# Gated delta stage of a two-block network: another spread of projections, norms and squares over a head, and two masked products for six copies

## The chip, the cores and the metric

The kernel runs on one core of a Trainium2 chip. The time is the device time of one execution in microseconds (us), the median of several runs. The core's engines have queues of their own and meet at semaphores: TensorE (PE, matrix products into eight PSUM banks), VectorE (DVE), ScalarE (ACT), GpSimd (POOL) and SyncE (SP, which issues the DMAs).

## The reference

The reference is a whole network of two blocks on 512 tokens of width 1024. The change is in one part of its first layer, the mixer with the gated delta rule. Four heads of width 128 each take four projections of the same input (query 0, key 1, value 2, gate 3). Query, key and value pass a causal convolution of four taps and a silu; query and key are brought to unit length; then the delta rule runs over four chunks of 128 tokens:

```python
g_qkv = jax.nn.silu(causal_dwconv(jnp.concatenate([g_q, g_k, g_v], -1), conv_g))
h_g = gated_delta_chunkwise(l2_norm(g_q), l2_norm(g_k), g_v, log_decay, beta)
y_g = head_rms_norm(h_g, g_norm) * jax.nn.silu(g_gate)

# in gated_delta_chunkwise, for each chunk
a_mat = where(strict, beta * kk * decay, 0) + eye        # unit lower triangular
sol = triangular_solve(a_mat, [v * beta, k * beta * exp(G)])
# and over the chunks
v_new = u - w @ state
o = q_dec @ state + attn @ v_new
state = g_last * state + k_dec.T @ v_new
```

## The kernel before

All work of the first layer's mixer is laid out by hand. `delta` (L2057) writes one list of instructions for each engine, and what order they have in the code is their order on the engine. Head h has a `body(h)` on each of PE, ACT, POOL and DVE (h = 0, 1, 2), and head 3 a `last_body`. While head h is solved and recurs, the next head (n = h + 1) is prepared and the one after (f = h + 2) is begun.

A projection is cut into eight units; one unit is the three 128x512 products of L190 to L192 (the float32 operands are split in a high and a low part). A head's body has two parts on PE:

- The levels. The triangular matrix is inverted blockwise, in six levels. A level has two short products, one into bank b4 (Y) and one into bank b6 (Z); ACT copies Y out of PSUM between them (`copy_y`), DVE takes Z up after them. Levels 1 to 4 work on 32x32 blocks (L2218), level 5 (`level_32`, L2239, L2248, L2249) on pairs of these, level 6 (`level_64`, L2256, L2262) on 64x64. These products are short and each waits for the other engines, so `fill(l, i)` puts units of other projections behind the Y product (i = 0) and behind the Z product (i = 1) of level l. For level 5 and 6 DVE first spreads the compact 32x32 blocks of T and U into the wide tiles `T_wide` and `U_wide` (L2701 four copies, L2703 two).
- The recurrence (`recur`), over four chunks, with `fill_chunk(c)` in the middle of chunk c.

Besides there are for the next head: `norms` (two 128x512 float32 products that sum squares, L2188, L2189), `roots` on ACT (four activations, L2424 to L2427), `unit` on DVE (L2666, L2667), `keys` on PE (key times key, key times query, key transposed, L2182, L2177), `scores` and `first_level` on DVE, and `turn_v` on PE (the value transposed).

Before the change, the gate projection of head n fills eight places in the levels (four for head 0), and the recurrence takes up query and key of head f and the value of head n, six units to a chunk. In head 2 there is no head f, so that only the value's eight units are left, two to a chunk. `norms` stand between levels 3 and 4, `keys` between level 6 and the recurrence. The squares for the norms are two activations of ACT. `split_high` (ACT, L154) and `split_low` (POOL, L163) split the weights of each projection in the two parts before it.

Of the kernel before, what the change touches and what calls it, by code (L numbers as in the profile page):

```python
# [20 lines left out]
P = 128  # L21
# [12 lines left out]
        ("reset", T), ("rcount", 2 * T), ("sel", 6 * P), ("small_levels", 32 * 5), ("small_ident", 32)]  # L34
# [2022 lines left out]
def delta(k, weights, out_tiles):  # L2057
# [23 lines left out]
     k_turned, v_turned, kdb_ready, vb_ready, kk_done, arg_ready, dec_ready, eg_ready, masked, at_ready, db_ready, qd_ready, t_ready, bt_ready, u_first, u_ready, a_ready, b0_ready, nat_ready, u_done, zeroed,  # L2081
# [3 lines left out]
         "k_turned v_turned kdb_ready vb_ready kk_done arg_ready dec_ready eg_ready masked at_ready db_ready qd_ready t_ready bt_ready u_first u_ready a_ready b0_ready nat_ready u_done zeroed "  # L2085
# [5 lines left out]
    order = [(0, 0), (1, 0), (2, 0), (3, 0), (0, 1), (1, 1)]  # L2091
    for h in range(H):
        order += [(s, g) for s, g in ((3, h + 1), (0, h + 2), (1, h + 2), (2, h + 1)) if g < H]
# [30 lines left out]

    def b_out(h):
        return b3 if h < H - 2 else b0 if h < H - 1 else b6

    def banks(h):

        return (b4, b5, b6) if h == 0 else (b0, b1, b2)  # L2130

    with nc.Block() as block:
# [19 lines left out]
        def _(pe):  # L2152
            def project(s, h, lo, hi):

                for m in range(lo, hi):
                    if m == 0:
                        k.wait_split(pe, seq[s, h])
                        if s == 3:
                            pe.wait_ge(gate_taken, h)
                            if h >= 3:  # L2160
                                pe.wait_ge(y_ready, h - 2)
                        elif s == 2:
                            pe.wait_ge(kdb_ready, h + 1)
# [27 lines left out]
            def keys(h):  # L2191
# [4 lines left out]
                if h:  # L2196
                    pe.wait_ge(vb_ready, h)
                turn(bt_, kk).then_inc(k_turned, 1)

            def turn_o(h):  # L2200
                pe.wait_ge(on_scaled, h + 1)
                if h == H - 1:
                    pe.wait_ge(s_ready, 3 * H)
                elif h == H - 2:
                    pe.wait_ge(masked, H)
                else:
                    pe.wait_ge(gate_taken, h + 3)
                turn(b_out(h), on).then_inc(o_turned, 1)

            def turn_v(h):  # L2210
                pe.wait_ge(v_silu, h + 1)
                turn(b2, v).then_inc(v_turned, 1)
# [39 lines left out]
            def level_64(h, fill):  # L2252
                A = Ats[h % 2]
                pe.wait_ge(nat_ready, h + 1)
# [5 lines left out]
                pe.wait_ge(y_copied, y_at(h, 6))  # L2260
                for c in range(NT):
# [36 lines left out]
            def mix(lo, hi):  # L2298

                for j, m in early_products[lo:hi]:  # L2300
                    if j == 0:
                        pe.wait_ge(*((y_ready, H - 1), (at_ready, H), (vb_ready, H), (gate_taken, H))[m])
# [6 lines left out]
            def body(h):  # L2309
                n, f = h + 1, h + 2  # L2310
                gate_slots = [(1, 0), (2, 0), (3, 0), (4, 0)] if n == 1 else [(1, 0), (1, 1), (2, 0), (2, 1), (3, 0), (4, 0), (5, 0), (6, 0)]
                chunk_units = [(s, g, m) for s, g in ((0, f), (1, f), (2, n)) for m in range(KD)]

                def fill(l, i):
# [3 lines left out]
                    if n < H and (l, i) in gate_slots:  # L2318
                        lo = gate_slots.index((l, i)) + KD - len(gate_slots)
                        project(3, n, lo, lo + 1)  # L2320

                def fill_chunk(c):
                    if f < H:
                        for s, g, m in chunk_units[6 * c:6 * c + 6]:
                            project(s, g, m, m + 1)
                    elif n < H:
                        project(2, n, 2 * c, 2 * c + 2)
                    else:
                        mix(11 + 2 * c, 13 + 2 * c)
# [11 lines left out]
                if n < H:  # L2341
                    norms(n)
                else:
# [7 lines left out]
                pe.wait_ge(zeroed, 2)  # L2351
                level_64(h, fill)
                fill(6, 1)
                if n < H:
                    keys(n)
# [18 lines left out]
        def _(act):  # L2374
# [22 lines left out]
            def silu_qk(h, i):  # L2397
# [6 lines left out]
                ch.link(nc.scalar.activation(qk[i][1][:, :], x[:, :], ACT.Silu))  # L2404
# [6 lines left out]
            def silu_gv(h):  # L2411
# [3 lines left out]
                nc.scalar.activation(gates[h % 3][:, :], gates[h % 3][:, :], ACT.Silu).then_inc(gate_done, 1)  # L2415
                act.wait_ge(v_conv, h + 1)
# [21 lines left out]
            def values(h):  # L2438
                act.wait_ge(v_turned, h + 1)
                for c in range(NT):  # L2440
                    ins = nc.scalar.activation(vb[:, cs(c)], b2[:, cs(c)], ACT.Copy, scale=col(2, h, c))
# [36 lines left out]
            def recur(h):  # L2478
# [3 lines left out]
                for c in range(NT):  # L2482
# [4 lines left out]
                    if c == 0:  # L2487
                        keys(n)
                    if c == 1:
                        if f < H:  # L2490
                            high(2, n)
                        if h:
                            normalize(h - 1)
                        if f < H:
                            tap(f, 0)
                    if c == 2:
                        high(3, f)
                        if f < H:
                            tap(f, 1)
                        else:  # L2500
                            out_tiles.split_high(act, 0)

            def body(h):
                n, f = h + 1, h + 2
                copy_y(h, 1)
                tap_v(h)
                silu_qk(n, 0)
                copy_y(h, 2)
                silu_qk(n, 1)
                square_qk(n, 0)  # L2510
                copy_y(h, 3)
                square_qk(n, 1)
                silu_gv(h)
# [3 lines left out]
                roots(n)  # L2517
                copy_y(h, 5)
                values(h)
                high(*((0, f) if f < H else (2, n)))  # L2520
                copy_y(h, 6)
                decay_query(n)
                high(1, f)
# [4 lines left out]
            def last_body(h):  # L2528
# [9 lines left out]
                silu_gv(h)  # L2538
# [45 lines left out]
        def _(pool):  # L2584
# [22 lines left out]

            def body(h):
                n, f = h + 1, h + 2
                if n < H:  # L2610
                    decays(n)
                low(*((0, f) if f < H else (2, n)))
                if n < H:
                    decayed(n)
                low(1, f)
                if n < H:
                    masks(n)
                if f < H:
                    low(2, n)
                low(3, f)  # L2620
# [872 lines left out]
```

## Time and profile before

| | |
|---|---|
| median of 3 runs | 1725.25 us (1725.08 to 1725.75) |
| the profiled execution | 1723.59 us, its span 1721.7 us |
| heads 0, 1, 2, 3 of the delta stage, in the span | 152.8, 201.9, 249.2, 287.2 to 320.6 us |
| PE busy over the span | 96% |

The span is from the first to the last instruction; times below are counted from its start. A head is counted from the first product of its level 1 to that of the next head. PE is the engine that is busy nearly all the time, and its granted clock is either full (2.4 GHz, shown as 1.00) or half of it (1.2 GHz, 0.50); the mean over a stretch says which part of it was at the lower level.

### The profile page before, as it was taken

To read this page: it belongs to the slowest core of one execution; us is meant where nothing else is said; L and a number is where in the kernel's file an instruction comes from. 1 tells how busy PE (TensorE), PEld (TensorE's weight loads), DVE (VectorE), ACT (ScalarE), POOL (GpSimd) and SP (SyncE) were. 2 spreads that over 40 slices of the span, in tenths; PEclk is the share of its full clock that TensorE was granted. 3 is DMA by queue.
4 is the path that set the end of the run, shared out by engine and by line. 5 is a ranking of instruction groups with operands and counts; after the bars stand their busy time and mean duration, and the time that the engine had idled before them with its cause. 6 is when DMAs were issued, how large, how long until landed. Compare 5 with 4: busy or idle time off the path is not lost. (4 is left out here: it accounts for less than half of the span.)

```text
span 1721.7 us, 25201 instructions
## 1 busy us (share of the span) xinstructions
PE 1659.1 (96%) x9050; PEld 1327.0 (77%) x9050; DVE 1052.4 (61%) x1720; ACT 842.2 (49%) x1433; POOL 408.0 (24%) x301
## 2 busy tenths in 40 slices
PE   9997997999999999989999999999999999999997
PEld 6785775778888878778888887888887876766775
DVE  6636444487666643587677748766664357888343
ACT  6756446354333332466656645433333245455673
POOL 1442322101111110035554630111111003232231
PEclk9998988999999999999999999999999999999999
DMA  5311112232333233312221212233323332221211
GB/s 217 125 61 63 50 38 69 93 97 87 97 94 93 94 98 97 110 49 62 74 64 60 74 50 102 83 97 97 96 87 98 97 110 63 100 74 62 61 62 49
DMA packets 40377, 144.43 MB, mean 84 GB/s; under 512 B 4562, under 2 KB 4818, under 8 KB 39780
## 3 DMA queue, kind: packets, MB, share of 16 engines
q1 hardware_dynamic: 40292, 143.30, 25.9%
q8 instruction: 54, 0.88, 0.2%
q14 instruction: 31, 0.25, 0.0%
HBM read 141.14 MB, written 2.13 MB: 83 GB/s over the span
## 5 line engine op out<-in xcount | busy, mean ns | idle before, releaser
L190 PE MATMUL bank<-u_high,w_high 128*128 128x512 f32 x1556 | 635.8, 409 | 11.0 <-ACT x_res L2449 2.7
L192 PE MATMUL bank<-u_high,w_low 128*128 128x512 f32 x1556 | 609.2, 392 | 0.0
L191 PE MATMUL bank<-u_low,w_high 128*128 128x512 f32 x1556 | 608.1, 391 | 0.0
L190 PEld LDWEIGHTS bank<-u_high,w_high 128*128 128x128 f32 x1556 | 293.0, 188 | 87.8 <-issue 25.3
L192 PEld LDWEIGHTS bank<-u_high,w_low 128*128 128x128 f32 x1556 | 292.9, 188 | 63.7
L191 PEld LDWEIGHTS bank<-u_low,w_high 128*128 128x128 f32 x1556 | 293.7, 189 | 57.1 <-issue 3.1
L154 ACT ACTIVATE w_high<-w_ring 128x1024 fp32r<-128x1024 f32 x228 | 238.9, 1052 | 185.6 <-PE bank L192 160.8
L163 DVE TENSOR_TENSOR w_low<-w_ring,w_high 128x1024 fp32r<-128x1024 f32 x175 | 221.4, 1270 | 159.8 <-ACT w_high L154 159.3
L163 POOL TENSOR_TENSOR w_low<-w_ring,w_high 128x1024 fp32r<-128x1024 f32 x53 | 127.4, 2409 | 340.9 <-ACT w_high L154 340.9
L928 ACT ACTIVATE conv_up<-bank,col_sb 128x512 f32<-128x512 f32 x88 | 68.7, 780 | 263.4 <-DVE bank L988 263.4
L1057 POOL TENSOR_TENSOR hidden<-conv_up 128x512 f32 x44 | 58.3, 1325 | 487.9 <-DVE conv_up L999 364.0
L190 PE MATMUL bank<-src_high_down,w_high 128*128 128x512 f32 x352 | 137.5, 391 | 3.4 <-DVE src_low_down L516 3.4
L988 DVE TENSOR_TENSOR bank<-bank,root_in 128x512 f32<-128x512 f32 x88 | 61.4, 697 | 127.3 <-PE bank L192 124.9
L192 PE MATMUL bank<-src_high_down,w_low 128*128 128x512 f32 x352 | 137.0, 389 | 0.0
L191 PE MATMUL bank<-src_low_down,w_high 128*128 128x512 f32 x352 | 137.0, 389 | 0.0
L1396 POOL TENSOR_TENSOR c_X<-c_k,c_dif 128x256 f32<-128x256 f32 x56 | 63.7, 1137 | 243.0 <-ACT c_dif L1287 243.0
L190 PEld LDWEIGHTS bank<-src_high_down,w_high 128*128 128x128 f32 x352 | 66.1, 188 | 19.3 <-issue 2.2
L192 PEld LDWEIGHTS bank<-src_high_down,w_low 128*128 128x128 f32 x352 | 66.1, 188 | 13.9
L998 DVE SCALAR_TENSOR_TENSOR conv_up<-bank,col_sb,conv_up 128x511 f32<-128x511 f32 x88 | 65.9, 749 | 17.7 <-ACT conv_up L928 13.5
L191 PEld LDWEIGHTS bank<-src_low_down,w_high 128*128 128x128 f32 x352 | 66.1, 188 | 13.5
L999 DVE SCALAR_TENSOR_TENSOR conv_up<-bank,col_sb,conv_up 128x510 f32<-128x510 f32 x88 | 65.9, 748 | 11.3 <-DVE conv_up L998 2.6
L1397 POOL TENSOR_TENSOR c_X<-c_q,c_dif 128x256 f32<-128x256 f32 x56 | 62.5, 1116 | 0.0
(442 smaller groups left out, 2113.6 us busy)
## 6 DMA issues: line engine op xcount, KB each, us to landing
w_ring<-ffn_up SPq DMA_DIRECT2D x88, 512.0 KB, 3.6
w_ring<-ffn_down SPq DMA_DIRECT2D x44, 512.0 KB, 3.6
w_ring<-c_in SPq DMA_DIRECT2D x32, 512.0 KB, 3.9
w_ring<-g_in SPq DMA_DIRECT2D x16, 512.0 KB, 3.7
w_ring<-m_in SPq DMA_DIRECT2D x12, 512.0 KB, 7.7
w_ring<-fox_in SPq DMA_DIRECT2D x12, 512.0 KB, 3.9
w_ring<-dsa_in SPq DMA_DIRECT2D x12, 512.0 KB, 3.6
w_ring<-ab_out SPq DMA_DIRECT2D x8, 512.0 KB, 4.1
```

What stands on the lines that cost most here:

```text
L154: self.nc.scalar.activation(self.ws[s][0][:, :], self.w[:, s, :], ACT.Copy).then_inc(self.w_high, 1)
L163: eng.tensor_tensor(low[:, :], self.w[:, s, :], high[:, :].bitcast(F32), ALU.subtract).then_inc(self.w_split, 1)
L190: nc.tensor.matmul(out, a[0], b[0], start=start, stop=False)
L191: nc.tensor.matmul(out, a[0], b[1], start=False, stop=False)
L192: return nc.tensor.matmul(out, a[1], b[0], start=False, stop=stop)
L928: nc.scalar.activation(cg[:, s, :], bank(i, s)[:, :], ACT.Identity, bias=coef(4 * i + s, 3), scale=coef(4 * i + s, 2)).then_inc(tap_done, 1)
L988: nc.vector.tensor_tensor(bank(i, s)[:, :], bank(i, s)[:, :], k.rn[:, :], ALU.mult).then_inc(taken, 1)
L998: ch.link(nc.vector.scalar_tensor_tensor(cg[:, s, 1:T], bank(i, s)[:, 0:T - 1], coef(4 * i + s, 1), cg[:, s, 1:T], ALU.mult, ALU.add))
L999: nc.vector.scalar_tensor_tensor(cg[:, s, 2:T], bank(i, s)[:, 0:T - 2], coef(4 * i + s, 0), cg[:, s, 2:T], ALU.mult, ALU.add).then_inc(con ...
L1057: nc.gpsimd.tensor_tensor(h[:, bass.ds(2 * i + s // 2, 1), :], cg[:, s - 1:s, :], cg[:, s:s + 1, :], ALU.mult).then_inc(mul_done, 1)
L1396: nc.gpsimd.tensor_tensor(x[:, :, 0, :], blocks(kk[:, :], b)[:, :, 0, :], d[:, :, 0, :], ALU.mult)
L1397: nc.gpsimd.tensor_tensor(x[:, :, 1, :], blocks(q[:, :], b)[:, :, 1, :], d[:, :, 1, :], ALU.mult).then_inc(x_ready, 1)
```

## The change

- On PE the levels now take up gate and value of head n, gate first, 12 of the 16 units (11 of 12 in head 0), and the rest of the value stands in chunk 0 of the recurrence (one unit to a chunk in head 2). Chunks 1 to 3 take query and key of head f, 5, 5 and 6 units. `norms` stand inside level 5, between Y and Z; `keys` stand at the end of chunk 0.
- The key of head n is taken and convolved on DVE at level 1 of head h (in head 0 its own value), and the value of head n in the recurrence. `unit` stands behind level 6.
- The squares move from ACT to POOL, and `roots` on ACT from before `copy_y` of level 5 to before that of level 6.
- The transposed value has bank b5 and the transposed key bank b3, before both b2.
- The wide tiles are made by two products with a mask of 32x32 blocks on the diagonal (128 more columns of constants) in place of six copies, and T_wide's lower block comes before those of U_wide. The two memsets of the wide tiles go.

```diff
+    def spread(x, n=P):
+        return x[0:n, :].rearrange("p (c a j) -> p c a j", a=1, j=B).to_broadcast([n, NT, n // B, B])
...
-        return (b4, b5, b6) if h == 0 else (b0, b1, b2)
+        return (b4, b5, b6) if h == 0 else (b0, b1, b3)
...
             def body(h):
                 n, f = h + 1, h + 2
-                gate_slots = [(1, 0), (2, 0), (3, 0), (4, 0)] if n == 1 else [(1, 0), (1, 1), (2, 0), (2, 1), (3, 0), (4, 0), (5, 0), (6, 0)]
-                chunk_units = [(s, g, m) for s, g in ((0, f), (1, f), (2, n)) for m in range(KD)]
+                units = [(s, n, m) for s in (3, 2) for m in range(KD)]
+                slots = {(1, 0): 1, (1, 1): 1, (2, 0): 2, (2, 1): 1, (3, 0): 1, (3, 1): 1, (4, 0): 1, (5, 1): 2, (6, 0): 1, (6, 1): 1}
+                if h == 0:
+                    units, slots[2, 0] = units[4:], 1
+                chunk_units = [(s, f, m) for s in (0, 1) for m in range(KD)]
...
                 def fill(l, i):
...
+                    if n < H:
+                        give(slots.get((l, i), 0))
+                    if n < H and (l, i) == (5, 0):
+                        norms(n)
...
                 def fill_chunk(c):
...
+                    elif f == H:
+                        give(1)
+                    elif c == 0:
+                        give(len(units))
+                    else:
+                        for s, g, m in chunk_units[5 * c - 5:5 * c if c < 3 else None]:
+                            project(s, g, m, m + 1)
+                    if n < H and c == 0:
+                        keys(n)
...
+            def square(h, i):
+                pool.wait_ge(qk_silu, 2 * (h - 1) + i + 1)
+                pool.wait_ge(nrm_qk, h)
+                x = qk[i][1]
+                ins = nc.gpsimd.tensor_tensor(k.sq[:, i, :], x[:, :], x[:, :], ALU.mult)
...
                 if n < H:
+                    square(n, 0)
+                    square(n, 1)
                     decays(n)
-                low(*((0, f) if f < H else (2, n)))
+                if h == 0:
+                    low(0, 2)
+                low(1, f)
...
                 if l == 4:
...
-                    for r in range(P // B):
-                        nc.vector.tensor_copy(wide(Un)[rows(r), :, rows(r)], small(Uc[rows(r), :]))
-                    for r in range(HP // B):
-                        nc.vector.tensor_copy(Tn[rows(r), :, rows(r)], small(Tc[rows(r), :]))
+                    nc.vector.tensor_tensor(Tn[0:HP, :, :].rearrange("p c (a j) -> p c a j", j=B), spread(Tc, HP), diagonal(HP), ALU.mult)
+                    nc.vector.tensor_tensor(Un[:, :].rearrange("p (c a j) -> p c a j", a=P // B, j=B), spread(Uc), diagonal(), ALU.mult).then_inc(wide_set, 1)
...
             def body(h):
                 n, f = h + 1, h + 2
-                take(h, 2)
+                last = (n, 1) if h else (0, 2)
+                take(*last)
                 level(h, 1)
-                convolve(h, 2)
+                convolve(*last)
                 level(h, 2)
                 decays(n)
                 level(h, 3)
                 level(h, 4)
-                unit(n)
                 level(h, 5)
                 take_gate(n)
                 level(h, 6)
+                unit(n)
+                if f < H:
+                    take(n, 2)
+                state(h, 0)
                 scores(n)
```

On PE, from level 6 of head 1 to its first chunk, before (L2256 and L2262 are the level, L2182 and L2177 the keys, L2270 and L2280 the start of the recurrence):

```order
L2256 MATMUL bank<-g_T_wide,x_res 64x64 x4
L190 MATMUL bank<-u_high,w_high 128x512
L191 MATMUL bank<-u_low,w_high 128x512
L192 MATMUL bank<-u_high,w_low 128x512
L2262 MATMUL bank<-g_U_wide,g_Y_wide 64x64 x4
L2182 MATMUL bank<-g_k 128x128 x4
L2182 MATMUL bank<-g_q,g_k 128x128 x4
L2177 MATMUL bank<-cst_sb,g_k 128x128 x4
L2270 MATMUL bank<-g_U_wide,x_res 128x128 x3
L2280 MATMUL bank<-g_vb,g_U_wide 128x128
```

The same place after the change (L2265 and L2272 are the level, L2280 and L2290 the start of the recurrence, L2190 the keys, which come behind four units in chunk 0):

```order
L2265 MATMUL bank<-g_T_wide,x_res 64x64 x4
L190 MATMUL bank<-u_high,w_high 128x512
L191 MATMUL bank<-u_low,w_high 128x512
L192 MATMUL bank<-u_high,w_low 128x512
L2272 MATMUL bank<-g_U_wide,g_Y_wide 64x64 x4
L190 MATMUL bank<-u_high,w_high 128x512
L191 MATMUL bank<-u_low,w_high 128x512
L192 MATMUL bank<-u_high,w_low 128x512
L2280 MATMUL bank<-g_U_wide,x_res 128x128 x3
L2290 MATMUL bank<-g_vb,g_U_wide 128x128
...
L2190 MATMUL bank<-g_k 128x128 x4
```

A unit has come between level 6 and the recurrence, and the keys have moved behind it.

On DVE, between level 4 and level 6 of head 1, before (L2701, L2703 the six copies, L2666, L2667 `unit`, L2706, L2707 level 5, L2647 the gate, L2709 level 6):

```order
L2701 COPY g_U_wide<-g_U 32x4x32 x4
L2703 COPY g_T_wide<-g_T 32x4x32 x2
L2666 TENSOR_TENSOR g_k<-g_k,g_rk 128x512
L2667 TENSOR_TENSOR g_q<-g_q,rstd 128x512
L2706 TENSOR_SCALAR g_U_wide<-bank 32x4x32 x2
L2707 TENSOR_SCALAR g_T_wide<-bank 32x4x32
L2647 TENSOR_TENSOR g_gate<-bank,root_in 128x512
L2709 TENSOR_SCALAR g_U_wide<-bank 64x4x64
```

And after it (L2748, L2749 the masked products, L2752, L2754 level 5, L2757 level 6, L2715, L2716 `unit`, L2692 the value):

```order
L2748 TENSOR_TENSOR g_T_wide<-g_T,cst_sb 64x256
L2749 TENSOR_TENSOR g_U_wide<-g_U,cst_sb 128x512
L2752 TENSOR_SCALAR g_T_wide<-bank 32x4x32
L2754 TENSOR_SCALAR g_U_wide<-bank 32x4x32 x2
L2696 TENSOR_TENSOR g_gate<-bank,root_in 128x512
L2757 TENSOR_SCALAR g_U_wide<-bank 64x4x64
L2715 TENSOR_TENSOR g_k<-g_k,g_rk 128x512
L2716 TENSOR_TENSOR g_q<-g_q,rstd 128x512
L2692 TENSOR_TENSOR bank<-bank,root_in 128x512
```

`unit` stands behind level 6 now, and T_wide's block (L2752) is the first of level 5.

On ACT, from level 4 to level 6 of head 1, before (L2470, L2473, L2475 the copies of Y, L2441 the scaled value):

```order
L2470 ACTIVATE g_Y<-bank 128x128
L2431 ACTIVATE g_dec<-g_dec 128x512
L2424 ACTIVATE rstd<-bank,eps_col 128x512
L2425 ACTIVATE g_rk<-bank,eps_col 128x512
L2426 ACTIVATE g_rk<-g_rk 128x512
L2427 ACTIVATE rstd<-rstd 128x512
L2473 ACTIVATE g_Y<-bank 32x128 x2
L2441 ACTIVATE g_vb<-bank,gate_cols 128x128 x4
L154 ACTIVATE w_high<-w_ring 128x1024
L2475 ACTIVATE g_Y_wide<-bank 64x256
```

And after it:

```order
L2494 ACTIVATE g_Y<-bank 128x128
L2455 ACTIVATE g_dec<-g_dec 128x512
L2497 ACTIVATE g_Y<-bank 32x128 x2
L2465 ACTIVATE g_vb<-bank,gate_cols 128x128 x4
L2448 ACTIVATE rstd<-bank,eps_col 128x512
L2449 ACTIVATE g_rk<-bank,eps_col 128x512
L2450 ACTIVATE g_rk<-g_rk 128x512
L2451 ACTIVATE rstd<-rstd 128x512
L2499 ACTIVATE g_Y_wide<-bank 64x256
```

The four roots have moved from before the copy of level 5 to before that of level 6.

## Rows read from the trace of the kernel before

**Rows 1.** The page: busy time, share of the span, instructions of each engine.
```profile
PE 1659.1 (96%) x9050; PEld 1327.0 (77%) x9050; DVE 1052.4 (61%) x1720; ACT 842.2 (49%) x1433; POOL 408.0 (24%) x301
```

**Rows 2.** Busy time by window, heads 0 to 2 (first figure length, then clock).
```profile
152.80:201.90 49.10, 42.20 (x468) 32.58 (x469) 23.36 (x52) 21.98 (x46) 17.07 (x14) 0.83 0.15 44
201.90:249.20 47.30, 43.52 (x481) 34.09 (x480) 22.71 (x51) 24.68 (x59) 15.15 (x11) 0.89 0.10 35
249.20:287.20 38.00, 31.41 (x433) 23.72 (x432) 16.98 (x43) 21.59 (x56) 10.39 (x9) 0.91 0.09 29
```

**Rows 3.** The same view, of the stretches of heads 0 to 2 at the lower clock.
```profile
156.00:166.20 10.20, 9.18 (x145) 4.78 (x138) 4.21 (x12) 6.66 (x11) 0.00 (x0) 0.50 0.01 2
173.00:179.80 6.80, 5.93 (x34) 5.65 (x35) 1.37 (x3) 1.96 (x3) 5.49 (x3) 0.50 0.27 78
217.40:227.60 10.20, 9.16 (x45) 8.21 (x46) 3.66 (x11) 3.23 (x12) 5.93 (x3) 0.50 0.01 2
265.20:272.00 6.80, 6.15 (x31) 5.20 (x32) 1.60 (x4) 2.18 (x10) 3.42 (x2) 0.50 0.45 154
```

**Rows 4.** Waits of PE, 125 to 320 us: releaser, us in total, times, longest.
```profile
PE bank L2256 <- DVE g_T_wide L2707: 8.1, 4, 2.5
PE bank L2218 <- ACT g_Y L2470: 3.1, 5, 1.1
PE bank L2248 <- ACT g_Y L2473: 3.0, 3, 1.6
PE bank L190 <- ACT x_res L2449: 2.7, 1, 2.7
PE bank L2218 <- DVE g_T L2694: 1.8, 2, 1.3
```

**Rows 5.** PE's timeline, heads 0 and 1: start, length, instruction.
```profile
146.76 1.16 PE L2182 MATMUL bank<-g_k 128*128 128x128 f32 x8 [1.51 <-DVE g_q L2667]
...
182.43 0.39 PE L190 MATMUL bank<-u_high,w_high 128*128 128x512 f32 x1
...
183.11 0.39 PE L190 MATMUL bank<-u_high,w_high 128*128 128x512 f32 x1
...
202.25 0.50 PE L190 MATMUL bank<-u_high,w_high 128*128 128x512 f32 x1
...
203.16 0.45 PE L2218 MATMUL bank<-g_Y,g_U 32*32 32x32 f32 x32
...
209.23 1.13 PE L2188 MATMUL bank<-sq,cst_sb 128*128 128x512 f32 x2
...
211.15 0.45 PE L2218 MATMUL bank<-g_T,g_BT 32*32 32x32 f32 x32
...
222.07 2.07 PE L2182 MATMUL bank<-g_k 128*128 128x128 f32 x8
```

**Rows 6.** DVE's timeline, head 1 from level 4 to level 5.
```profile
213.62 2.11 DVE L2701 COPY g_U_wide<-g_U 32x128 f32<-32x128 f32 x4
...
216.21 0.69 DVE L2666 TENSOR_TENSOR g_k<-g_k,g_rk 128x512 f32<-128x512 f32 x1
...
218.00 0.28 DVE L2707 TENSOR_SCALAR g_T_wide<-bank 32x128 f32<-32x128 f32 x1
```

**Rows 7.** ACT's timeline, head 1: the first root, and what follows the last.
```profile
212.37 0.68 ACT L2424 ACTIVATE rstd<-bank,eps_col 128x512 f32<-128x512 f32 x1
...
214.84 0.55 ACT L2473 ACTIVATE g_Y<-bank 32x128 f32<-32x128 f32 x2
215.41 1.14 ACT L2441 ACTIVATE g_vb<-bank,gate_cols 128x128 f32<-128x128 f32 x4
```

**Rows 8.** POOL and DVE at once: a product of DVE, POOL's product, a split.
```profile
144.89 1.27 POOL L2593 TENSOR_TENSOR g_dec<-g_dec,cst_sb 128x512 f32<-128x512 f32 x1 [4.02 <-ACT g_dec L2431]
144.93 1.78 DVE L2667 TENSOR_TENSOR g_q<-g_q,rstd 128x512 f32<-128x512 f32 x1
...
217.58 2.34 POOL L163 TENSOR_TENSOR w_low<-w_ring,w_high 128x1024 fp32r<-128x1024 f32 x1 [2.39 <-ACT w_high L154]
```

More of the change, by code:

```diff
@@ L2090, in delta @@
     k.clear_retired()
-    order = [(0, 0), (1, 0), (2, 0), (3, 0), (0, 1), (1, 1)]
-    for h in range(H):
-        order += [(s, g) for s, g in ((3, h + 1), (0, h + 2), (1, h + 2), (2, h + 1)) if g < H]
+    order = [(0, 0), (1, 0), (2, 0), (3, 0), (0, 1), (1, 1), (3, 1), (2, 1), (0, 2)]
+    for f in range(2, H):
+        order += [(s, g) for s, g in ((1, f), (3, f), (2, f), (0, f + 1)) if g < H]
     seq = {tile: n for n, tile in enumerate(order)}
@@ L2340, in body @@
                 fill(3, 1)
-                if n < H:
-                    norms(n)
-                else:
+                if n == H:
                     turn_v(h)
@@ L2403, in silu_qk @@
                 x = (qk1 if h == 1 else qk)[i][1]
-                ch.link(nc.scalar.activation(qk[i][1][:, :], x[:, :], ACT.Silu))
+                ins = nc.scalar.activation(qk[i][1][:, :], x[:, :], ACT.Silu)
+                if h:
+                    ins.then_inc(qk_silu, 1)
+                else:
+                    ch.link(ins)
             def square_qk(h, i):
@@ L2505, in body @@
                 copy_y(h, 1)
-                tap_v(h)
-                silu_qk(n, 0)
-                copy_y(h, 2)
-                silu_qk(n, 1)
-                square_qk(n, 0)
+                if h:
+                    tap(n, 1)
+                    silu_gate(h)
+                else:
+                    high(2, 1)
+                    tap_v(0)
+                    silu_qk(1, 0)
+                copy_y(h, 2)
+                if h:
+                    silu_v(h)
+                    silu_qk(n, 0)
+                else:
+                    silu_qk(1, 1)
+                    silu_gate(0)
                 copy_y(h, 3)
-                square_qk(n, 1)
-                silu_gv(h)
+                if h:
+                    silu_qk(n, 1)
+                else:
+                    silu_v(0)
                 nc.scalar.preload_act_table_set(LNEXP)
@@ L2516, in body @@
                 decays(n)
[L2517 removed]
                 copy_y(h, 5)
                 values(h)
[L2520 removed]
+                if h == 0:
+                    high(0, 2)
+                roots(n)
                 copy_y(h, 6)
+                high(1, f)
                 decay_query(n)
[L2523 removed]
                 if h:
@@ L2736, in body @@
                 level(h, 6)
+                unit(n)
+                if f < H:
+                    take(n, 2)
+                state(h, 0)
                 scores(n)
+                if f < H:
+                    convolve(n, 2)
+                state(h, 1)
                 first_level(n)
-                state(h, 0)
                 if f < H:
                     take(f, 0)
-                state(h, 1)
-                if f < H:
-                    convolve(f, 0)
-                    take(f, 1)
                 state(h, 2)
```

87 lines of the change are left out of this document (46 added, 41 removed).

## The prediction

> **What bounds the kernel now.** First the page: PE is busy for 96% of a span of 1721.7 us, so only what gives PE fewer waits, or a higher clock, can shorten it; the instructions of PE are the same before and after the change, 4203 rows of the order each. [rows 1] Then the windows, one for each of the heads 0 to 2 of the delta stage. PE's busy time falls short of the length by 6.9 us in head 0 (49.1 less 42.2), 3.8 in head 1 and 6.6 in head 2. Beside that the mean clock is 0.83, 0.89 and 0.91: with the two levels 1.00 and 0.50, PE was at 1.2 GHz for twice the missing part, 16.7 us of head 0, 10.4 of head 1, 6.8 of head 2. [rows 2] The windows of these stretches show PE busy nearly throughout, 9.18 of 10.2, 5.93 of 6.8, 9.16 of 10.2 and 6.15 of 6.8 us, at half speed. [rows 3] What came before them are the places where PE waited: the stretch at 217.4 us lies behind two waits of level 5 and 6. Who kept PE waiting is in the list of waits: T_wide before level 6 (8.1 us, at most 2.5 at once, so 2.5 in three heads and 0.5 in the fourth), the copies of Y (3.1 and 3.0), DVE's T (1.8, once 1.3, in levels 1 and 2 of head 0), and the scaled key x_res (2.7, once, in head 2: there the value's projection waits for ACT to have read the transposed key out of its bank b2). [rows 4]
>
> So two terms are to be had per head: the waits, and half of what was done at 1.2 GHz. That the second is real is seen on the keys: the same eight products take 1.16 us at 146.76 and 2.07 us at 222.07, inside such a stretch. [rows 3, 5]
>
> **The change part by part.** *The wait before level 6.* On DVE, level 4 of head 1 is followed by four copies (2.11 us from 213.62), two more, `unit` (two products of 0.69), and then level 5, whose last instruction starts at 218.00. [rows 6] Of this chain the six copies (to about 216.2) become two masked products. A product of 128x512 float32 with both inputs in SBUF takes 0.69 [rows 6], and in the one place where it met a POOL product of 1.27 us it took 1.78 [rows 8]; I take 0.4 and 0.7 us, with bounds 0.3 and 0.7 for each below and 1.78 each above. It does not decide: `norms` now stand between Y and Z of level 5, which gives DVE 1.92 us (209.23 to 211.15) [rows 5], and behind Z stand two units. A unit takes 0.68 us in a row of units (182.43 to 183.11). [rows 5] `unit` (1.3 us) is out of the chain altogether. So T_wide is there about 0.4 us behind Z and PE has 1.36 us of work: the wait of 2.5 us is gone in each head. If the masked products took 1.78 us both, they would end 3.6 us behind level 4, still before the end of `norms` plus the two units.
>
> *The copies of Y.* The copy of level 5 stood behind four roots on ACT, which took from 212.37 to 214.84. [rows 7] They now stand before the copy of level 6, with the four scalings of the value (1.14). [rows 7] From Y of level 5 that is about 0.6 for the copy, 1.1, and then the roots, which can't start before the norms are done at 1.9: 2.0 + 2.5 = 4.5. PE has norms 1.9, Z 0.5, two units 1.4, Y 0.6 and a unit 0.9, together 5.3. In heads 1 and 2 this hides the roots. In head 0 a weight split of ACT stands before them too, and PE waits about 0.5.
>
> *The squares.* POOL does each in about 1.27 us (its product of 128x512 with both inputs in SBUF [rows 8]), behind the silu of the key at level 3. From there to `norms` PE has some 3.5 us, for 1.3 + 0.1. POOL is idle there now in heads 1 and 2. In head 0 a split of 2.34 us stands before, and it is done before the first silu. I cost the squares at nothing; if they were late, every us would be PE's. ACT loses two squares, so that its copy at level 4 is 1.2 us earlier.
>
> *More units between short products.* A unit between two short products costs 0.91 us and not 0.68 (202.25 to 203.16) [rows 5]; where PE would wait anyway this is free. Head 0 has some six such places more, heads 1 and 2 two: 1.4, 0.5, 0.4 us lost.
>
> *Keys inside chunk 0.* Behind level 6 PE has one unit, the start of the recurrence (0.8), and in chunk 0 four units in head 1, one in heads 0 and 2, before it wants `unit`'s result: 4.3 us in head 1, 2.3 in heads 0 and 2. DVE needs 0.5 for level 6 and 1.3 for `unit`, 1.9 with the semaphores. It is hidden if nothing holds DVE. In heads 0 and 1 POOL begins a weight split of 2.34 us [rows 8] just there: ACT's part of it stands behind the copy of level 6 and ends about as DVE gets to `unit`. The one meeting of the sort in the trace: DVE's product started 0.04 us behind POOL's of 1.27 and took 1.78, that is 1.1 more than alone, POOL's whole remainder. [rows 8] So `unit` is done at 1.9 in the best case and at 4.2 in the worst. In head 1 that is hidden either way, in head 0 it costs 0 to 1.9; I take 1.7, since both are released by the same copy and POOL's is the longer.
>
> The Trainium skill (SBUF — State Buffer, "Who interferes with whom") says that a VectorE instruction with two SBUF inputs and a GpSimd instruction that reads SBUF exclude each other for a whole instruction, and that the order of issue decides. The row at 144.93 us agrees; by the page the cost in head 0 is either nothing or POOL's remainder, nothing in between, and the sum would be 1.7 us better if DVE came first.
>
> *New waits in the recurrence.* Query of head f goes into bank b0, where the keys' product now lies until `scores` has read it: from the end of the keys PE has about 1.4 us and DVE needs 1.75, so 0.35 in heads 0 and 1. In head 2 ACT's eight scalings of the key (2.1 us) stand before the copy of v_new of chunk 1, and PE has 1.9 us: about 0.5; the normalising and `first_level` in chunks with one unit may add 0.3. In return the wait of 2.7 us for b2 in head 2 is gone, since the key is turned into b3. Further small waits: 0.4 in each.
>
> *Level 1 and 2 of head 0.* DVE is still behind with the second head's key there, so level 2 starts at the same time as before; the unit more fills 0.9 us of a wait of 1.3 [rows 4], and the copy at level 2, held by the loading of the silu table on ACT, ends when it did: PE, with less to do, waits 1.4 instead of 0.5.
>
> *The clock.* Where the waits go the stretches at 1.2 GHz should go. Half of the busy time of rows 3 is 4.6 + 3.0 in head 0, 4.6 in head 1, 3.1 in head 2. In head 0 waits of 0.4 and 1.4 us remain near the place where the clock fell before, so I keep one stretch of some 3.4 us of work there, 1.7 us lost.
>
> Sum over waits, clock and slots. Head 0: waits 6.9 less 4.4 that remain or are new (0.4 + 1.4 + 0.5 + 1.7 + 0.4), plus 7.6 less 1.7 of clock, less 1.4 = 7.0. Head 1: 3.8 less 0.75, plus 4.6, less 0.5 = 7.1. Head 2: 6.6 less 1.2, plus 3.1, less 0.4 = 8.1. Head 3 keeps its order; its list of instructions before level 6 gets shorter by the copies and its T_wide comes first, for a wait of 0.5 us: 0.5. Together 22.7 us. The profiled execution took 1723.59 us, so 1700.9; the median of the runs shown is 1.66 above it, and I state **1702.6 us** for the median.
>
> **What could go otherwise.** (a) *Head 0 stays slow.* For: the clock fell at 156 us behind the wait of 1.3 us [rows 4] and stayed down for 10.2 us though PE was busy for 9.18 of them [rows 3]; the waits that I leave in head 0 are of this size, and `unit` may cost a second fall in chunk 0. Against: levels of this density in head 1 ran at full clock up to 217.4. It would cost half of some 7 to 10 us more, so a gain of 18 to 19 and 1706. (b) *The waits change place.* Squares late on POOL, the copy of level 6 late behind the roots, `unit` behind the split, and DVE's four scalings of `decays`, which meet a square: 1.5 us per head, and each again followed by a stretch at half clock. This would keep about half of the gain, 11 us, so 1714. For: all four engines get tighter rows than before. Against: each has 0.3 to 2 us to spare by the sums above. (c) *Slower than before: the clock in the levels.* The change moves 4 to 7 units of each head out of the recurrence, where PE ran without a wait, into the levels. If the many short products with single units between them were granted 1.2 GHz throughout, then levels of 17 to 18 us of work in three heads would cost 17 us each. Against: head 1 ran eight units in its levels at the full clock. It decides from 22.7 us lost, that is from 45 us of added time at half clock (before: 34 in heads 0 to 2); with all three heads, 51 us lost, 1731. (d) *It does nothing*: the waits of heads 0 to 2 are on PE itself and each has its releaser in the change, so I see only the case that all come back, 1725.
>
> **Chances.** The forecast 0.57, with its own range 1699.5 to 1704.5. (a) 0.25, (b) 0.13, (c) 0.03, (d) 0.02. The range that holds 8 of 10 reaches from 1698.5 (the masked products, `unit` and the clock of head 0 all at their better bounds, 1.7 + 1.7 + a little) to 1709, which takes in (a). The gain is 20 times what a measurement can tell from no change, about 0.2% or 3.5 us. Faster by more than that 0.94, within it 0.03, slower 0.03.
>
> **What would show it.** In the list of waits, PE on T_wide before level 6 gone or under 0.5 us in all, and the wait for x_res gone. Heads of 42, 40 and 30 us. The mean clock of heads 1 and 2 at 1.00, that of head 0 at 0.95. A wait of PE for DVE's `unit` in head 0 alone, and beside it a DVE product of more than 1.5 us while POOL splits weights. The norms not waiting for POOL. I am wrong if PE's busy time in heads 1 and 2 doesn't fall by more than 3 us each (then the clock did not come back), or if waits for POOL, or for ACT at level 6, stand at the head of PE's list.

## The result and the profile after

| | before | after |
|---|---|---|
| median, same chip | 1725.50 us (1725.08 to 1730.70, 4 runs) | 1696.78 us (1695.93 to 1698.30, 4 runs) |
| the profiled execution, its span | 1723.59, 1721.7 us | 1695.94, 1694.0 us |
| heads 0, 1, 2, 3, each to the next | 49.1, 47.3, 38.0, 33.2 us | 38.3, 39.6, 29.2, 32.3 us |

The ratio is 0.9828, with a 95% interval of 0.9807 to 0.9848: 28.7 us faster by the medians. The forecast was 1702.6 with a range from 1698.5, so the gain is larger than forecast by 6 us and the time lies below the range. The direction and the places were right; the size of head 0 was not.

The page of the changed kernel, its line for PE, and the windows of its four heads (length, then busy time of PE, its weight loads, DVE, ACT and POOL, then the granted clock, the busy share of the DMA engines and GB/s):

```profile
PE 1648.5 (97%) x9050; PEld 1317.2 (78%) x9050; DVE 1050.1 (62%) x1704; ACT 838.7 (50%) x1427; POOL 417.3 (25%) x305
```

```profile
152.43:190.76 38.33, 36.63 (x465) 27.74 (x465) 22.68 (x48) 22.60 (x46) 25.32 (x18) 1.00 0.22 63
190.76:230.37 39.61, 39.61 (x481) 30.35 (x480) 22.01 (x47) 22.69 (x56) 17.25 (x13) 1.00 0.15 46
230.37:259.53 29.16, 28.74 (x433) 21.18 (x432) 16.17 (x39) 19.41 (x53) 9.79 (x10) 1.00 0.06 24
259.53:291.84 32.31, 28.16 (x416) 20.82 (x416) 17.38 (x33) 19.54 (x46) 1.02 (x2) 0.95 0.33 107
```

Head 3 of the kernel before, in the same view:

```profile
287.20:320.40 33.20, 28.11 (x416) 20.86 (x416) 17.62 (x37) 19.58 (x46) 0.03 (x1) 0.95 0.31 104
```

Set against [rows 2]: PE has as many instructions as before over the whole execution (9050), but in the heads 0 to 2 the mean clock is 1.00 in place of 0.83, 0.89 and 0.91, and busy time is length in head 1 without a gap. The four differences are 10.8, 7.7, 8.8 and 0.9 us, together 28.2 us, where the span is shorter by 27.7. Head 0 also starts 0.4 earlier, and 0.9 is lost behind head 3, in stages whose instructions the change does not touch.

While PE works, two stretches at half clock are left, of 3.4 us each, one in head 3 and one at some 746 us; in the delta stage before there were five, 37.4 us in all [rows 3, and one of 3.4 us in head 3]. The first window lies where the clock of head 0 fell before, the others over the two stretches that are left (the last two begin a little before the fall, so that they show a mean between 0.50 and 1.00):

```profile
156.40:159.80 3.40, 2.20 (x70) 1.34 (x69) 2.96 (x6) 2.57 (x6) 2.24 (x3) 1.00 0.51 154
267.90:271.30 3.40, 3.40 (x71) 2.23 (x70) 0.88 (x3) 2.62 (x4) 0.00 (x0) 0.60 0.02 5
745.70:749.10 3.40, 2.85 (x12) 2.56 (x13) 1.14 (x4) 0.23 (x1) 3.40 (x5) 0.61 0.49 154
```

The waits of PE in the changed kernel, 125 to 320 us (releaser, us in total, times, longest), to be laid beside [rows 4]:

```profile
PE bank L2227 <- ACT g_Y L2494: 2.6, 3, 1.2
PE bank L190 <- DVE y_mix L2770: 1.8, 1, 1.8
PE bank L2190 <- DVE g_q L2716: 1.5, 1, 1.5
...
PE bank L2227 <- DVE g_T L2737: 0.8, 1, 0.8
...
PE bank L2300 <- ACT g_vn L2508: 0.4, 1, 0.4
PE bank L2227 <- DVE g_T L2743: 0.4, 1, 0.4
```

The waits for T_wide (8.1 us), for the copy of level 5 (3.0) and for x_res (2.7) are gone, and none on POOL has come. The 1.5 us for `unit` (g_q) stand at 146 us, ahead of head 0, and were there before the change too [rows 5]. PE's timeline of head 0 shows where waits are left: in level 2, and a gap of 0.13 us before Z of level 6 (L2272); there is none before its Y (L2265) and none before the keys (L2190).

```profile
155.42 0.45 PE L2227 MATMUL bank<-g_T,g_BT 32*32 32x32 f32 x32 [0.37 <-DVE g_T L2743]
...
157.97 0.45 PE L2227 MATMUL bank<-g_Y,g_U 32*32 32x32 f32 x32 [1.20 <-ACT g_Y L2494]
...
168.29 0.67 PE L2265 MATMUL bank<-g_T_wide,x_res 64*64 64x64 f32 x8
...
169.99 0.68 PE L2272 MATMUL bank<-g_U_wide,g_Y_wide 64*64 64x64 f32 x8
...
172.99 1.05 PE L2190 MATMUL bank<-g_k 128*128 128x128 f32 x8
```

DVE in the same head, the masked products and `unit`:

```profile
164.27 0.48 DVE L2748 TENSOR_TENSOR g_T_wide<-g_T,cst_sb 64x256 f32<-64x256 f32 x1
164.68 0.68 DVE L2749 TENSOR_TENSOR g_U_wide<-g_U,cst_sb 128x512 f32<-128x512 f32 x1
...
171.04 0.68 DVE L2715 TENSOR_TENSOR g_k<-g_k,g_rk 128x512 f32<-128x512 f32 x1
171.64 0.68 DVE L2716 TENSOR_TENSOR g_q<-g_q,rstd 128x512 f32<-128x512 f32 x1
```

And POOL beside it, a square, the product of the decays that met the masked ones, and the split that met `unit`:

```profile
157.83 1.04 POOL L2650 TENSOR_TENSOR sq<-g_q 128x512 f32<-128x512 f32 x1 [1.16 <-ACT g_q L2422]
...
164.55 1.93 POOL L2632 TENSOR_TENSOR g_db<-g_dec,delta_bc 128x512 f32<-128x512 f32 x1
...
171.10 3.46 POOL L163 TENSOR_TENSOR w_low<-w_ring,w_high 128x1024 fp32r<-128x1024 f32 x1 [1.44 <-ACT w_high L154]
```

None of the four DVE products was held by more than 0.06 us: 0.48 (0.42 in head 3, where POOL is idle) and 0.68, 0.68 and 0.68. POOL was, both times: the split took 3.46 where it takes 2.34 alone [rows 8]. So the case that I priced at 1.7 us fell the other way. By the profile's records DVE's product began at 171.04 and POOL's at 171.10, but that these 0.06 us decided it is not shown: in head 1 the split's record begins 0.31 us ahead of `unit`'s (207.85 against 208.16), and there too `unit` takes 0.68 twice and the split 3.83.

### The profile page after: what moved, and what is told of

It reads as the page before. It is cut to its first block and busy times, and to the rows that moved or that the text cites. A ratio compares the mean times of both kernels' runs of the same rounds, so it can differ in the third digit from the quotient of the medians.

```text
span 1694.0 us, 25191 instructions
## 1 busy us (share of the span) xinstructions
PE 1648.5 (97%) x9050; PEld 1317.2 (78%) x9050; DVE 1050.1 (62%) x1704; ACT 838.7 (50%) x1427; POOL 417.3 (25%) x305
```

## The experiments

Ratios are to the kernel before on the same chip. The changed kernel itself has 0.9828 (0.9807 to 0.9848). The runs of the experiments were taken apart from its own, on several chips, so that differences of a microsecond or two between two medians are not told apart.

**Six copies back** (the changed kernel with the old way of spreading, the memsets included):

```diff
+   nc.gpsimd.memset(Un[:, :], 0.0).then_inc(zeroed, 1)
+   nc.gpsimd.memset(Tn[:, :, :], 0.0).then_inc(zeroed, 1)
...
-   nc.vector.tensor_tensor(Tn..., spread(Tc, HP), diagonal(HP), ALU.mult)
-   nc.vector.tensor_tensor(Un..., spread(Uc), diagonal(), ALU.mult)
+   for r in range(P // B):
+       nc.vector.tensor_copy(wide(Un)[rows(r), :, rows(r)], small(Uc[rows(r), :]))
+   for r in range(HP // B):
+       nc.vector.tensor_copy(Tn[rows(r), :, rows(r)], small(Tc[rows(r), :]))
```

> The changed kernel, with the six copies and the two memsets back in place of the two masked products; nothing else. Theory (the norms inside level 5 are the cover, the masked products are not needed): the copies take about 2.6 us behind level 4 of each head, as against 1.1 now, and end about when Z of level 5 does; PE's wait for T_wide before level 6 stays under 0.3 us, the clock stays at 1.00, and the time is within 0.7 us of the changed kernel's 1696.8. Rival (the masked products bring the gain): the wait of 2.5 us before level 6 is back in three heads, 7.5 us, and half-clock stretches behind it: 1704 or more.

Measured: 1697.69 (1695.97 to 1700.39), ratio 0.9843 (0.9819 to 0.9867), not to be told from the changed kernel, though 0.2 us outside the 0.7 that I had allowed. There is no wait on T_wide in it, and the rival (1704 or more) is out. DVE in head 1:

```profile
201.75 2.10 DVE L2753 COPY g_U_wide<-g_U 32x128 f32<-32x128 f32 x4
203.86 0.44 DVE L2755 COPY g_T_wide<-g_T 32x128 f32<-32x128 f32 x2
204.41 0.28 DVE L2759 TENSOR_SCALAR g_T_wide<-bank 32x128 f32<-32x128 f32 x1
```

The copies cost 2.54 us against 1.16 for the masked products, and are covered by `norms`, which stand in level 5 now, and the units behind Z. With the new order around them the masked products are worth 0.9 us by the medians and 2.6 by the ratios, both within the noise.

**The masked products alone** (the kernel before, its order kept, with the two masked products of the change in place of the six copies):

> The kernel before, with the two masked products in place of the six copies; nothing else. Theory: DVE's chain before level 6 is shorter by about 1.4 us (2.56 to 1.1), so PE's wait there falls from 2.5 to about 1.1 us in heads 0 to 2, 4 us in all. If the clock falls as before the time is 1720 to 1722; if the clock holds in heads 1 and 2 because the wait is short, another 5 to 8 us: 1713 to 1716. Rival (POOL's products of decays hold the masked ones up): the wait stays over 2 us and the time within 1 us of before.

Measured: 1721.83 (1719.41 to 1724.66, 10 runs), ratio 0.9982 (0.9971 to 0.9994): 2.4 us of gain by the medians. The head of PE's list of waits, and DVE in head 1:

```profile
PE bank L2262 <- DVE g_T_wide L2712: 6.6, 4, 2.0
PE bank L2224 <- ACT g_Y L2476: 3.9, 5, 1.3
```

```profile
211.39 0.49 DVE L2706 TENSOR_TENSOR g_T_wide<-g_T,cst_sb 64x256 f32<-64x256 f32 x1
211.80 0.68 DVE L2707 TENSOR_TENSOR g_U_wide<-g_U,cst_sb 128x512 f32<-128x512 f32 x1
212.62 1.54 DVE L2672 TENSOR_TENSOR g_k<-g_k,g_rk 128x512 f32<-128x512 f32 x1
```

DVE saves 1.4 us on the spreading and gives 0.9 back one instruction later: `unit` now meets POOL's decay product (211.68, 1.93 us) and takes 1.54. The wait falls by 0.5 per head, from 2.5 to 2.0, where I had expected 1.1, and the clock falls in heads 0 to 2 as before, for example

```profile
217.60:224.40 6.80, 6.80 (x34) 6.03 (x33) 2.36 (x5) 2.36 (x10) 3.68 (x3) 0.50 0.00 0
```

So the order is what gains: 26.5 us by the medians of six_copies, over nine tenths of the whole, against 2.4 for the masked products alone. The two add up to the 28.7 of the whole change, so that no extra gain from having both is to be seen.

**More work in the waits** (the kernel before with extra products of PE, into a bank that nobody reads, in its places of waiting):

```diff
+   if n < H and (l, i) == (5, 1):
+       dummy(9)
+   if n == 1:
+       dummy({(1, 1): 4, (2, 1): 1, (5, 0): 5, (6, 0): 1}.get((l, i), 0))
```

> The kernel before, its order kept, with extra products of 128x512 into an unused bank put where PE waits in the levels: nine before level 6 in heads 0 to 2 (2.0 us of a wait of 2.5), and in head 0 also four at level 1, one at level 2, five at level 5, one at level 6. Their results are not used. Theory (the half-clock stretches are behind the waits, and cost half of the work in them): the places where PE waits stay as late as before, but the clock is 1.00 in heads 1 and 2 and higher in head 0, and the time falls by 5 to 13 us, to 1712 to 1720, though PE got more to do. Rival (the clock falls for the many short products, not for the waits): clock as before, time the same or up to 3 us longer.

Measured: 1715.10 (1712.31 to 1716.84), ratio 0.9936 (0.9914 to 0.9959). PE does more work and the kernel is 9.1 us faster by the medians. Its heads 0 to 2, by windows:

```profile
154.09:198.91 44.82, 42.69 (x485) 32.27 (x485) 23.64 (x52) 21.97 (x46) 17.11 (x14) 0.96 0.16 48
198.91:242.05 43.14, 41.62 (x491) 31.97 (x490) 22.63 (x51) 24.68 (x59) 15.21 (x11) 1.00 0.11 38
242.05:278.72 36.67, 32.33 (x442) 24.27 (x441) 16.91 (x43) 21.64 (x56) 10.41 (x9) 0.95 0.09 30
```

The clock is 0.96, 1.00 and 0.95 where it was 0.83, 0.89 and 0.91 [rows 2], with the releasers untouched: the waits were not shortened, only filled. What came back is the half of the stretches that are gone. I had expected 1.00 in head 2 as well. There the wait of 2.7 us for x_res got no filling, and a stretch at half clock stands behind it. So the two terms of the prediction are separate, and the second is real.

**Part of the value out of the levels** (the changed kernel with the gate alone in the levels, eight slots or four in head 0, and the whole value in the recurrence):

```diff
-   slots = {(1, 0): 1, (1, 1): 1, (2, 0): 2, (2, 1): 1, (3, 0): 1, (3, 1): 1, (4, 0): 1, (5, 1): 2, (6, 0): 1, (6, 1): 1}
+   slots = {(1, 0): 1, (1, 1): 1, (2, 0): 1, (2, 1): 1, (3, 0): 1, (3, 1): 1, (4, 0): 1, (5, 1): 1}
...
-                    units, slots[2, 0] = units[4:], 1
+                    units = units[4:]
+                    slots = {(1, 0): 1, (2, 0): 1, (3, 0): 1, (4, 0): 1}
...
-                        give(1)
+                        give(2)
```

> The changed kernel with the value's projection taken out of the levels: 8 units in the levels (4 in head 0), the rest in chunk 0 of the recurrence (two to a chunk in head 2). Theory (the units in the levels fill waits, and the clock falls where waits are long): PE waits at level 6 for ACT's copy behind the roots (about 1 to 2 us, more in head 0) and for DVE before the recurrence (0.7), so 2 to 3 us a head in heads 1 and 2 and 4 or more in head 0; the clock falls in head 0 and perhaps in the others. 1702 to 1709, with the clock below 1.00 in at least one head. Rival (the new places of norms, keys and unit alone bring the gain): under 1699, no wait over 0.7 us.

Measured: 1711.11 (1709.33 to 1713.11), ratio 0.9918 (0.9894 to 0.9941), 14 us slower than the changed kernel and 2 above the range that I had given. Its heads 0 to 2, and the largest waits of PE:

```profile
152.37:200.48 48.11, 42.46 (x465) 32.33 (x465) 22.91 (x48) 22.75 (x46) 24.60 (x18) 0.82 0.16 50
200.48:242.01 41.53, 39.58 (x481) 30.42 (x480) 22.23 (x47) 22.68 (x56) 16.91 (x13) 1.00 0.15 44
242.01:274.09 32.08, 30.06 (x433) 22.52 (x432) 16.35 (x39) 19.41 (x53) 10.79 (x10) 0.95 0.06 21
```

```profile
PE bank L2227 <- ACT g_Y L2495: 3.5, 5, 1.2
PE bank L2272 <- ACT g_Y_wide L2500: 3.4, 3, 1.3
PE bank L2227 <- DVE g_T L2744: 2.3, 3, 1.3
```

Half of the gain hangs on the four to seven units more per head, and two thirds of that half on head 0: it takes 48.1 us in place of 38.3, of which 4.0 are longer waits and 5.8 more busy time, at a mean clock of 0.82 in place of 1.00. The copy of level 6 behind the roots is late by up to 1.3 us here: that is the wait I expected at half a microsecond in head 0, and the units of level 5 and 6 are what covers it.

**Keys before the recurrence** (the changed kernel, `keys(n)` back behind level 6):

> The changed kernel with the keys' products back between level 6 and the recurrence. Theory: DVE's unit is done about 1.9 us behind level 6 and PE has one unit of 0.7 us until then: a wait of 1.1 us before the keys in heads 0 to 2, 3.4 us in all, the clock held: 1699.5 to 1701; with a fall of the clock up to 1704. Rival (the place of the keys is indifferent): within 0.7 us of 1696.8.

Measured: 1700.11 (1699.37 to 1700.43), ratio 0.9858 (0.9843 to 0.9873). PE waits on `unit` in each head now, 3.9 us in all where it was 1.5:

```profile
PE bank L2190 <- DVE g_q L2716: 3.9, 4, 1.5
```

The 2.4 us of waits come back as 3.3 us of time, and the clock stays up. So the keys' place is worth about 3 us by the medians (5 by the ratios, whose intervals still touch).

**Squares on ACT** (the changed kernel, `square` as two activations behind the silus):

> The changed kernel with the squares on ACT again, each behind its silu, and off POOL. Theory (ACT had room): the copy of Y at level 4 is up to 0.2 us later, DVE's four scalings take 0.8 instead of 1.5 us, and the time is within 0.7 us of 1696.8. Rival (the squares on ACT hold up the copies): 0.6 to 1.2 us of wait more at levels 3 and 4 of each head, 1699 or more.

Measured: 1697.58 (1697.37 to 1698.37), ratio 0.9845 (0.9830 to 0.9860): 0.8 us above the changed kernel's median, not to be told from it, and the list of PE's waits in the delta stage is the same. ACT has room for both, and POOL too. The one thing that moves is DVE's `decays`, 0.83 us for four instructions here and 1.48 where POOL's square (158.83) runs beside them; PE waits for neither.

**The split thrice** (the changed kernel, POOL doing head 0's split of query 2 three times, so that POOL is busy before `unit` starts):

> The changed kernel, with POOL's split of the query weights of head 2 done three times over in head 0 (the same values again), so that POOL is in the middle of a product of 2.4 us when DVE comes to unit at about 171.0 us. Theory (whoever began first keeps the ports for its instruction; in the changed kernel DVE came first by a few hundredths): DVE's first product of unit takes 1.5 to 1.9 us instead of 0.68, and PE waits about 0.5 us before the keys of head 0. Rival (DVE is not held by a split, or goes first whoever began): both products take 0.68 us and POOL's split gets longer.

Measured: 1698.14, one run, span 1696.3 against 1694.0; head 0 took 40.97 us against 38.33. DVE's `unit` and POOL:

```profile
171.31 1.62 DVE L2718 TENSOR_TENSOR g_k<-g_k,g_rk 128x512 f32<-128x512 f32 x1
172.85 2.84 DVE L2719 TENSOR_TENSOR g_q<-g_q,rstd 128x512 f32<-128x512 f32 x1
```

```profile
167.53 4.85 POOL L2665 TENSOR_TENSOR w_low<-w_ring,w_high 128x1024 fp32r<-128x1024 f32 x2 [0.78 <-ACT w_high L154]
172.46 5.45 POOL L163 TENSOR_TENSOR w_low<-w_ring,w_high 128x1024 fp32r<-128x1024 f32 x2
```

The products take 1.62 and 2.84 in place of 0.68 each, and PE waits 2.3 us before the keys. So the step of the prediction (POOL first, `unit` held for POOL's remainder, PE waits) does happen when POOL is in the middle of a product, and costs more than I had, since both products were held. In the changed kernel it does not occur.

**Fewer waits** (the changed kernel, aimed at what its list of waits shows: ACT's tap of head 1's query before the decays at the start, and in head 3 the value's tap and projection earlier):

```diff
             roots(0)
+            tap(1, 0)
             decays(0)
-            tap(1, 0)
...
+                tap_v(h)
                 normalize(h - 1)
-                tap_v(h)
...
-  early_products = [(0, 1), (0, 3), (0, 0), (1, 1), (1, 3), (1, 0), (0, 2), (1, 2), ...]
+  early_products = [(0, 1), (0, 3), (0, 2), (1, 1), (1, 3), (1, 2), (0, 0), (1, 0), ...]
...
-  closing = {(1, 2): 0, (3, 2): 1, (5, 2): 2}
+  closing = {(1, 0): 0, (3, 2): 1, (5, 2): 2}
```

> The changed kernel with three moves more: at the start ACT taps head 1's query before it computes the decays of head 0, so that POOL's product doesn't meet DVE's second product of unit (1.8 us instead of 0.7); in head 3 the value is tapped before the output of head 2 is normalised, and the first products into the query's bank stand behind those into the value's, so that PE doesn't wait 1.8 us for the output of head 2. Theory: 1.1 us at the start, 1.8 us in head 3, and 1.7 us of the half-clock stretch behind that wait: 1692 to 1693.5. Rival (the waits come back one place later): 1696 to 1697.

Measured: 1692.18 (1691.58 to 1695.30, 5 runs), ratio 0.9811 (0.9798 to 0.9825), as forecast. It is 4.6 us under the changed kernel's median; the intervals of the two ratios overlap, but all five runs lie below the fastest of the changed kernel (1695.93). The wait on y_mix (1.8) is gone, with the stretch at half clock behind it, and the wait before the first keys is 0.4 in place of 1.5. The profiled execution was the slowest of the five, 1695.30, and it shows a part of why: the 1.20 us wait of level 2, which the changed kernel has too, is followed here by a stretch at half clock, which costs about 1.6 us, half of the 3.23 that PE was busy in it. The rest of the 3.1 us above the median stays open, as the faster executions left no trace.

```profile
156.57 0.65 PE L2227 MATMUL bank<-g_Y,g_U 32*32 32x32 f32 x32 [1.20 <-ACT g_Y L2494]
```

```profile
156.40:159.80 3.40, 3.23 (x68) 2.36 (x69) 2.18 (x7) 1.51 (x5) 2.04 (x2) 0.53 0.44 140
```

Compare the row at 157.97 above: the same product behind the same wait took 0.45 us at full clock.

**Copy first** (fewer_waits, and in head 0 ACT's copy of level 2 before the silu whose table load of 1.28 us held it):

```diff
                     tap_v(0)
+                copy_y(h, 2)
+                if h == 0:
                     silu_qk(1, 0)
-                copy_y(h, 2)
```

> This is the kernel of fewer_waits with one more order changed: in head 0 ScalarE copies the Y of level 2 before it does the silu of the next head's query and key sums, whose table load stood ahead of that copy. Theory (what is left to gain in head 0 is the 1.20 us wait of TensorE on that copy, and the clock that fell behind it in one profiled execution of fewer_waits): VectorE's product for T is then the later of the two and starts after its own convolution work, so the wait falls by only about 0.3 us; with the clock held through head 0 the time is 1691 to 1692.5 us, at or slightly under the 1692.2 of fewer_waits. Rival (the table load only moves, and stands ahead of the copy of level 3 then): the time is 1692.5 to 1694 us, with a wait of about 1 us at level 3 in the place of the one at level 2.

Measured: 1692.19 (1691.87 to 1694.42), ratio 0.9810 (0.9796 to 0.9824), the same as fewer_waits. The 1.20 us wait is gone and one of 0.46 on DVE's T stands in its place:

```profile
157.71 0.45 PE L2227 MATMUL bank<-g_T,g_BT 32*32 32x32 f32 x32 [0.46 <-DVE g_T L2744]
```

No stretch of half clock is left in the four heads of this execution. By the traces head 0 is 0.65 us shorter than in the changed kernel (37.68 against 38.33), and in this execution a wait of 1.7 us for the very first weights (0.7 at the most in the changed kernel's) took that back; the medians do not tell the two kernels apart. What I expected in the wait (0.3 less) was too little, what I expected in time was in the range.

## Why the prediction was right in its places and short in its size

- *T_wide before level 6*, predicted gone: held. But the prediction gave the masked products and the move of `norms` in one account; six_copies shows that `norms` and the units behind Z together cover six copies as well. How the worth of the order divides among the moves of `norms`, of `roots` and of the banks was not run.
- *The heads 1 and 2*, predicted 7.1 and 8.1: measured 7.7 and 8.8. The clock came back in full, as in the sum. The waits that I had left there (0.75 and 1.2) were 0.0 and 0.4; the 0.4 is the wait for the copy of v_new in head 2 that I had at 0.5. I had also written that I am wrong if PE's busy time in these heads doesn't fall by more than 3 us each. It fell by 3.9 and by 2.7. The sign was badly set, since my own sum for head 2 has 3.1 less 0.4, that is 2.7; the mean clock of 1.00 shows that the clock did come back.
- *Head 0*, predicted 7.0: measured 10.8, and this is where the prediction failed. Waits: 6.9 less 4.4 was the sum; length less busy time is now 1.7 (38.33 less 36.63). Of the five terms in the 4.4 two were right, T of level 2 (0.4; measured 0.37) and its copy (1.4; measured 1.20). "`unit` held behind the split, 1.7" was nothing: POOL was the one held (3.46), and `unit` took 0.68 twice. Why DVE went first stays open; its record begins 0.06 us ahead of POOL's, but in head 1 POOL's is ahead of `unit`'s by 0.31 and DVE goes first as well. The copy of level 6 (0.5) cost 0.13: the roots ran from 167.07, the copy from 169.56 for 0.38, the unit ended at 169.86, and Z began at 169.99. The small ones (0.4) were nothing. Together 2.7 us too pessimistic.
- *The clock in head 0*: I kept one stretch, 1.7 us lost. In the profiled execution there was none (1.00 throughout). The waits before it are as forecast; what was wrong is to take a fall as certain behind a wait of such size. Six traces have this wait of 1.2 us with the same units around it: the clock held in five (the changed kernel, six_copies, keys_before, squares_act, split_thrice) and fell in one (fewer_waits). What decides between the two stays open.
- *More units between short products*: 1.4 predicted in head 0. Busy time fell by 5.57 where the clock alone gives 7.6, so the slots cost 2.0; 0.6 worse than forecast. These three, 2.7 + 1.7 less 0.6, are head 0's 3.8.
- *Head 3*: 0.5 predicted, 0.9 measured.
- *The squares on POOL at nothing*: held; 1.04 us each where I had 1.27, and squares_act makes no difference.
- *The rivals*: (a), that head 0 stays slow, did not come: its clock is 1.00. (b), that the waits change place, is what value_in_chunk0 does (1711.1, near the 1714 I had for it), but with fewer units in the levels, not with these. (c) did not come: levels full of short products with single units between ran at 1.00. Its price of 1731 was also wrongly added, since 51 us lost on top of 1702.6 give 1754.
- *The size of the gain against the noise*: 22.7 us is 6 to 7 times the 3.5 us that I gave as what a measurement can tell, not 20 times.
- *The range*: its low end allowed 1.7 for `unit` and 1.7 for the clock, but not that the half microseconds beside them vanish too, and the small gains in heads 1 to 3 add in the same direction. Most were cost terms that I had set above nothing though their cover was nearly equal to their length.

## What to carry to other kernels

Where PE alternates between short dependent products and waits, count a wait twice: its length, and half of the work done at half clock behind it; the test is to fill the waits with useless products, and if the kernel gets faster, the clock was part of the loss (9.1 us here, of the 28.7 of the whole change). Put independent units and the sums that are due anyway in the places where PE waits rather than speeding up the step that it waits for: once the order was right, the faster spreading was not measurable. When two engines that exclude each other are released within a tenth of a microsecond, price both orders and keep both in the range's ends, and don't add up such costs at their bad ends for the forecast itself.

## What the runs showed of the hardware that I had not expected

- DVE's two products back to back kept POOL out over both. POOL's split began 0.06 us behind the first and took 3.46 in place of 2.34, 1.1 more, where the remainder of the first product was 0.6. In head 1 it began 0.04 behind DVE's last work of level 6 (207.81, one input from a PSUM bank) and 0.31 ahead of `unit`, and took 3.83, and both `unit` products after it 0.68. With POOL ahead the two engines took turns instead: 1.62 and 2.84. The Trainium skill (SBUF — State Buffer, "Who interferes with whom") has the exclusion and that who starts first holds the pair of SBUF ports that the two share for the whole instruction. The traces agree with that for single meetings (1.78 against 1.27 in [rows 8]), and show beside it that the engine that waits does not always get the next turn, and in head 1 that the one whose record begins first is not always the one that goes first; which rule decides it stays open. Where the page and these traces differ, the traces count.
- POOL can be lengthened without PE ever waiting for it: the decay product took 1.93 beside the masked products, and 1.27 in six_copies, where the copies stand in their place.
- A POOL product of 128x512 with one tensor as both inputs takes 1.04 us, with two tensors 1.27.
- The granted clock after the same wait differs between executions of nearly the same program (0.45 and 0.65 us for the product at level 2). The runs of one kernel differ by 1 to 5 us; how much of that is the clock is not shown. A later stage shows the same at some 745 us, behind a wait of 2.4 us for POOL: at half clock in the changed kernel and in masked_only, at full clock in the profiled execution of before. I did not settle what decides it.
